# Two stacked transformer blocks on one core: the full stop between projections and recurrence of each later layer taken out, its semaphores cleared in two groups instead

## What is computed

```python
def second_block(x, ...):
    for l in range(DEPTH_2):                                   # 2 layers
        h = rmsnorm(x, g_pre_mix[l])
        y = token_mixer(h, w_in[l], ...)
        x = x + rmsnorm(y, g_post_mix[l])
        h = rmsnorm(x, g_pre_ffn[l])
        y = conv_ffn(h, w_up[l], ffn_conv_w[l], w_down[l])
        x = x + rmsnorm(y, g_post_ffn[l])

def token_mixer(h, w_in, ...):
    z = h @ w_in
    mq, mk, mv, mo, mif, aq, ak, av = split(z)
    qk = silu(causal_dwconv([mq, mk], qk_conv_w) + qk_conv_b)
    log_i, log_f = gates(mif + gate_bias)
    ht = mlstm(q, k, v=mv, log_i, log_f)                       # recurrence with decays
    m_out = rms(ht) * mh_norm_g * sigmoid(mo)
    a_out = sliding_window_attention(rope(aq), rope(ak), av, sinks)
    return [m_out, a_out] @ w_out
```

## Time and profile before

| what | us |
|---|---|
| median of 3 executions | 2817.95 |
| lowest and highest | 2817.07, 2821.88 |
| the profiled execution | 2818.63 |
| its span, first to last instruction | 2816.8 |
| PE busy in the span | 2639.3 (94%) |
| DVE, ACT, POOL busy | 1213.9, 878.8, 848.7 |

### The profile page before, as it was taken

How to read it: one execution, slowest core, us unless ns; L and a number is a source line. 1 busy time by engine, 2 the same in 40 slices (tenths; PEclk the granted TensorE clock), 3 DMA queues, 4 the chain that set the end, 5 groups by cost and what they waited for, 6 DMA issues and landing times.

```text
span 2816.8 us, 36700 instructions
## 1 busy us (share of the span) xinstructions
PE 2639.3 (94%) x14324; PEld 1881.7 (67%) x14324; DVE 1213.9 (43%) x2417; ACT 878.8 (31%) x1666; POOL 848.7 (30%) x1166
## 2 busy tenths in 40 slices
PE   8999999999988888888888899999999999999998
PEld 8997777888533333333333367788888887788887
DVE  4333735314733333333333357553341565643422
ACT  3343334323211111111111144543332445433332
POOL 4343343553000000000000043335555435355454
PEclk9999999999999999999999999999999999999999
DMA  4222221335999999999999951122232221122322
GB/s 147 90 91 96 85 74 54 109 105 195 392 427 427 428 428 429 428 429 429 428 429 428 426 177 64 57 90 90 90 104 106 88 98 60 60 90 93 117 90 75
DMA packets 128007, 572.26 MB, mean 203 GB/s; under 512 B 11136, under 2 KB 58624, under 8 KB 102784
## 3 DMA queue, kind: packets, MB, share of 16 engines
q1 hardware_dynamic: 122624, 561.09, 50.2%
q10 hardware_dynamic: 5248, 9.32, 1.1%
HBM read 566.12 MB, written 4.26 MB: 202 GB/s over the span
## 4 chain that ended last, share of the span: by engine, by line
PE 67%; DMA 22%; DVE 6%; ACT 2%; issue 1%; POOL 1%; SPq 0%; POOLq 0%; DVEq 0%; ACTq 0%
PE ps L390 41%; DMA wide<-in_moe_w 15%; PE ps L1462 8%; DMA arena<-in_moe_w 7%; PE ps L1942 4%; PE ps L1921 3%; PE ps L1909 1%; PE ps L1962 1%; PE ps L640 1%; PE ps L604 1%; PE ps L1928 1%; POOL ring_r L347 1%; PE ps L619 1%; PE ps L1242 1%; PE ps L859 0%
## 5 line engine op out<-in xcount | busy, mean ns | idle before, releaser
L347 POOL TENSOR_TENSOR ring_r<-ring,ring_r 128x256 fp32r<-128x256 f32 (+2 forms) x1136 | 830.0, 772 | 1871.7 <-ACT ring_r L330 1871.7
L390 PE MATMUL ps<-xnT_r,ring_r 128*128 128x512 f32 (+1 forms) x1664 | 483.9, 374 | 0.0
L390 PE MATMUL ps<-ring_r,xnT_r 128*128 128x512 f32 (+1 forms) x1360 | 439.3, 394 | 8.1 <-POOL ring_r L347 2.5
L390 PEld LDWEIGHTS ps<-xnT_r,ring_r 128*128 128x128 f32 x1664 | 304.5, 188 | 56.7 <-issue 1.3
L390 PE MATMUL ps<-ring_r,arena_r 128*128 128x512 f32 x1392 | 327.9, 394 | 0.0
L390 PEld LDWEIGHTS ps<-ring_r,xnT_r 128*128 128x128 f32 x1360 | 285.6, 222 | 51.3 <-issue 7.1
L390 PE MATMUL ps<-xn_r,ring_r 128*128 128x512 f32 (+1 forms) x832 | 310.2, 373 | 0.0
L390 PEld LDWEIGHTS ps<-ring_r,arena_r 128*128 128x128 f32 x1392 | 263.1, 190 | 58.8 <-issue 3.7
L330 ACT ACTIVATE ring_r<-ring 128x1024 fp32r<-128x1024 f32 (+2 forms) x284 | 272.1, 1025 | 93.4 <-DMA ring<-in_w_down 69.4
L1942 PE MATMUL ps<-wide,arena 128*32 128x512 f32 x768 | 203.6, 678 | 92.2 <-DMA wide<-in_moe_w 92.2
L1942 PEld LDWEIGHTS ps<-wide,arena 128*32 128x32 f32 x768 | 55.3, 121 | 237.4 <-issue 237.4
(11 more groups left out here) (386 smaller groups left out, 3475.1 us busy)
## 6 DMA issues: line engine op xcount, KB each, us to landing
wide<-in_moe_w SPq DMA_DIRECT2D x143, 2048.0 KB, 32.9
arena<-in_moe_w SPq DMA_DIRECT2D x47, 2048.0 KB, 32.9
ring<-in_w_in SPq DMA_DIRECT2D x22, 2048.0 KB, 8.3
ring<-in_w_up SPq DMA_DIRECT2D x20, 2048.0 KB, 8.6
ring<-in_w_down SPq DMA_DIRECT2D x10, 2048.0 KB, 7.9
ring<-in_w_in SPq DMA_DIRECT2D x16, 512.0 KB, 4.9
ring<-in_w_out SPq DMA_DIRECT2D x4, 2048.0 KB, 8.3
ring<-in_w_ret_branch SPq DMA_DIRECT2D x2, 2048.0 KB, 8.2
```

The costliest lines, as they stand in the source:

```text
L347: ins = nc.gpsimd.tensor_tensor(ring_r[:, q % 2, piece], ring[:, q % 2, piece], ring_r[:, 2 + q % 2, piece].bitcast(F32), ALU.subtract)
L390: ins = nc.tensor.matmul(bank, left, right, start=(start and k == 0), stop=(stop and k == 2))
```

## The change

The stage semaphores that the later layers use are put in two groups, PROJECTING (34 names, those of the projections) and MIXING (33 names, those of the recurrence and the feed-forward part); the rest is never cleared again. The stop is gone. POOL clears the group that is not in use, twice for each layer but the first:

- in l = 1, after first_low_pool and ahead of the low halves of unit 1, it clears MIXING. It waits until PE has made the second chunk of the first job, ACT has drained behind the second turned tile, and DVE has drained behind enter_dve;
- in both layers, after the low halves of unit 6 and ahead of those of unit 7, it clears PROJECTING, when the three engines have each counted early in the recurrence.

At the start of the recurrence PE now waits for single banks and values instead: rotated keys kept, the last job in bank 7 and in banks 0 and 1 taken, the silu of q and k done, and the low half of the turned attention output. DVE waits for the sigmoid and drains behind the first decay mask, ACT waits for DVE's last taking and drains behind its first exp. wait_cleared (a wait and a count) stands at the head of each part, for groups that were cleared long before.

```diff
-        def next_stage(eng, me, chain=None):
...
-                for done in stage_done.values():
-                    eng.wait_ge(done, n + 1)
-                eng.sem_inc(stage_left, 1)
-                eng.sem_clear(range(nums[0], nums[-1] + 1))
-                eng.drain().then_inc(stage_open, 1)
-            else:
-                eng.drain().then_inc(stage_done[me], 1)
-                eng.wait_ge(stage_open, n + 1)
-                eng.sem_inc(stage_left, 1)
...
+        def clear_left(pool, n, group):
+
+            for done in stage_done.values():
+                pool.wait_ge(done, n)
+            pool.sem_inc(stage_left, 1)
+            pool.sem_clear(group)
+            pool.drain().then_inc(stage_open, 1)
+
+        def wait_cleared(eng, n):
+
+            eng.wait_ge(stage_open, n)
+            eng.sem_inc(stage_left, 1)
...
@@ chunk_pe
+            elif n == 0 and c == 1 and current["l"]:
+                ins.then_inc(stage_done["pe"], 1)
...
@@ project_dve
             enter_dve(v, link)
+            if current["l"]:
+                v.drain().then_inc(stage_done["dve"], 1)
             v.wait_ge(layer_loaded, (current["l"] + 1) * (16 * LAYER_ROWS))
...
@@ project_act
+                    if k == 1 and current["l"]:
+                        a.drain().then_inc(stage_done["act"], 1)
...
@@ a_product_pe
             if c == 0 and n >= 2:
                 pe.wait_ge(V.taken_act, n - 1)
+            elif c == 0:
+                projected_bank_taken(pe, n)
...
+            elif n == 2 and c == 0:
+                ins.then_inc(stage_done["pe"], 1)
...
@@ mlstm_pe
                 elif what == "decays":
                     if k >= 2:
                         pe.wait_ge(Z.strip_ready, k - 1)
+                    elif k:
+                        projected_bank_taken(pe, DECAY_BANKS[1])
+                    else:
+                        pe.wait_ge(Z.turned_kept, 2 * NT)
...
                     if done:
                         pe.wait_ge(V.scores_taken, done)
+                    else:
+                        pe.wait_ge(qk_silu_done, 1)
+                        pe.wait_ge(Z.out_low, NT)
...
@@ mlstm_dve, diagonal
+                if n == 0:
+                    v.wait_ge(mo_sigmoid_done, 1)
+                    v.drain().then_inc(stage_done["dve"], 1)
...
@@ mlstm_act
+            a.wait_ge(Z.taken_dve, max(taken_count(n) for n in range(len(J.order)) if not by_act(n)))
             nc.scalar.activation(floor, floor, ACT.Exp).then_inc(V.exp_ready, 1)
+            a.drain().then_inc(stage_done["act"], 1)
...
@@ the order of POOL
                 if l:
                     first_low_pool(pool)
-                for q in (1, 2, 3, 4, 5):
+                    clear_left(pool, 2 * l + 1, mixing_nums)
+                for q in range(1, Q_UP):
                     low_pool(pool, q)
-                nxt()
-                for q in range(6, LAYER_UNITS):
+                clear_left(pool, 2 * l + 2, projecting_nums)
+                for q in range(Q_UP, LAYER_UNITS):
                     low_pool(pool, q)
```

More of the change, by code:

```diff
@@ L181, in build @@
         STAGE = [
[L182 to L192, removed]
@@ L193, in build @@
-            "x_turned", "x_kept",
-            "act_high", "act_low", "block_used", "attended", "half_gated", "rows_normed", "x_returned", "routes_loaded", "merge_asked", "merge_ready", "out_turned", "out_kept", "out_low", "head_done", "x_low", "ff_ready", "ff_weighted", "ff_taken", "ff_gated", "ff_done",
+            "dve_chain", "act_chain", "expert_x_kept", "last_products", "last_kept", "last_added", "spill_done", "spill_open", "gate_ready",
+            "silu_ready", "up_ready", "hidden_ready", "down_ready", "gate_kept", "up_kept", "gate_summed", "up_summed", "gate_turned",
@@ new lines, in build @@
+            "up_turned", "y_act", "y_dve", "shifted", "picked", "picks_ready", "gated_ready", "gathered", "picks_turned", "picks_kept", "united",
+            "tile_united", "spill_x_kept", "logits_ready", "gains_ready", "spilled_out", "spilled_in", "half_gated", "rows_normed", "x_returned",
+            "routes_loaded",
+        ]
+        PROJECTING = [
+            "attended", "biased", "exp_asked", "exp_ready", "max_ready", "mixed_ready", "mixed_taken", "out_kept", "out_low", "out_turned",
+            "probs_kept", "probs_ready", "probs_turned", "proj_ready", "ranked", "roots_ready", "roped", "rows_ready", "scores_ready",
+            "scores_taken", "sums_ready", "taken_act", "taken_dve", "tile_added", "turned", "turned_kept", "weighted", "x_kept", "x_low",
+            "x_turned", "merge_asked", "merge_ready", "gated", "chosen",
+        ]
@@ L195, in build @@
+        MIXING = [
+            "act_high", "act_low", "block_used", "deviation", "ff_ready", "ff_weighted", "ff_taken", "ff_gated", "ff_done", "head_done",
+            "moments", "strip_asked", "strip_ready", "tile_down", "turned_low",
         ]
@@ L199, in build @@
         ]
-        STAGE += ["later_" + name for name in LATER]
+        MIXING += ["later_" + name for name in LATER]
+        STAGE += PROJECTING + MIXING
         for name in STAGE:
@@ L209, in build @@
         decay_row_ready, queries_weighed = (stage_sems[n] for n in ("ff_gated", "ff_done"))
+        projecting_nums = range(stage_sems[PROJECTING[0]].num, stage_sems[PROJECTING[-1]].num + 1)
+        mixing_nums = range(stage_sems[MIXING[0]].num, stage_sems[MIXING[-1]].num + 1)
+        qk_silu_done, mo_sigmoid_done = stage_sems["gated"], stage_sems["chosen"]
         spill_known = sem("spill_known")
@@ L2538, in layers_sp @@
                     load_small_rows(sp, l + 1)
+            wait_cleared(sp, 2 * LAYERS)
             for i in range(NT):
@@ L2804, in project_act @@
                     if q == Q_MO and i == NT - 1:
-                        nc.scalar.activation(Y.qk, Y.qk, ACT.Silu)
+                        nc.scalar.activation(Y.qk, Y.qk, ACT.Silu).then_inc(qk_silu_done, 1)
                     if q == Q_MV and i == 0:
                         a.wait_ge(Z.taken_act, NT)
-                        nc.scalar.activation(Y.mo, Y.mo, ACT.Sigmoid)
+                        nc.scalar.activation(Y.mo, Y.mo, ACT.Sigmoid).then_inc(mo_sigmoid_done, 1)
                 elif what == "scores":
@@ L2918, in build, with projected_bank_taken @@
         M_TURN_BANK = 7
+        def projected_bank_taken(pe, bank):
+            wait_job_taken(pe, max(n for n in range(len(J.order)) if dense_bank(n) == bank))
         def a_product_pe(pe, n, c):
@@ L3023, in mlstm_pe @@
                         pe.wait_ge(V.mixed_taken, k)
+                    else:
+                        pe.wait_ge(Z.mixed_taken, NT)
                     for i in range(NT):
@@ L3537, in _ @@
                 current["l"] = l
+                if l:
+                    wait_cleared(pe, 2 * l)
                 project_pe(pe)
-                nxt()
+                if l:
+                    wait_cleared(pe, 2 * l + 1)
                 mlstm_pe(pe)
@@ L3560, in _ @@
                 current["l"] = l
+                if l:
+                    wait_cleared(v, 2 * l)
                 project_dve(v, link)
-                nxt()
+                if l:
+                    wait_cleared(v, 2 * l + 1)
                 mlstm_dve(v, link)
@@ L3565, in _ @@
                 down_split_dve(v)
+            wait_cleared(v, 2 * LAYERS)
             last_dve(v, link)
@@ L3619, in _ @@
                 current["l"] = l
+                if l:
+                    wait_cleared(a, 2 * l)
                 project_act(a)
-                nxt()
+                if l:
+                    wait_cleared(a, 2 * l + 1)
                 mlstm_act(a)
@@ L3625, in _ @@
                 down_split_act(a)
+            wait_cleared(a, 2 * LAYERS)
             last_act(a)
```

17 lines of the change are left out of this document (removed).

## The result

| | median us | lowest, highest | ratio to before, 95% interval |
|---|---|---|---|
| before | 2817.99 | 2817.07, 2821.88 | |
| the changed kernel | 2829.32 | 2827.74, 2832.05 | 1.0039 [1.0029, 1.0049] |

The change makes the kernel 0.39% slower; the medians differ by 11 us. The profiled execution of the changed kernel took 2827.84 us with a span of 2825.7.

A forecast was written before the change was run, and what follows sets the result against it. PE was taken to bound the kernel (two thirds of the span), most of the rest being the first block's expert weights. Stops -7.8 and hold +10.8 gave +3.0 us: median 2821.0 us, range 2817.5 to 2826.0.

The forecast's parts named there:

- rival 3: At the recurrence the new waits end as late as the removed stop, which gives nothing: 2828.8 us; chance 0.05.
- No second stall.: In l = 1, behind the first AKV job, POOL is ahead again with QK (11.35 us for four quarters); no cost added.
- POOL's pace: In l = 1, POOL's sixteen AKV pieces behind the new clear take 8.1 us.
- The stops, -7.8: Removing the stops at the recurrence in l = 0 and l = 1 gives 3.9 us each; bounds -3.7 and -7.8.
- Rival 1: Behind the missing stops PE's clock stays low, so two give 3.7 us, not 7.8: 2825.0 us; chance 0.19.
- The hold, +10.8: In l = 1 the new clear holds POOL ahead of AKV: +8.5 late, +2.3 of clock, bounds 8.7 to 12.7.
- the quick end: In l = 1, POOL's sixteen AKV pieces beside an idle DVE take 7.9 us, making the sum 0.2 us lower.
- The clock's 2.3 us: In l = 1, around PE's wait for AKV, half clock costs +2.3 us, bounds 0.7 and 3.4.
- Rival 2: POOL or PE slack hides the wait ahead of AKV in l = 1; only stops count: 2810.2 us; chance 0.09.

The follow-up runs named there:

- the three variants: Changed kernel with the l = 1 clear of MIXING behind QK, behind unit 5, or behind QK plus PSUM operand: 2815.80, 2813.57, 2812.31 us.
- the two kernels without the long add: Changed kernel with the keys' sine term in PSUM, or with POOL pausing ahead of QK until DVE's first AKV rotary step: 2820.62, 2821.11 us.

## Why the prediction was wrong, step by step

The time, 2829.3, lies above the range of 2817.5 to 2826.0. Of the chances, slower by over 0.2% had 0.30; it came, but not by the mechanism that I had given it. That rival 3's 2828.8 lies near the measured time is chance: its mechanism, a stop under another name, is not in the profile.

**The step that failed is "No second stall."** I asked whether POOL's pieces of QK would be in time for PE, and they were. I didn't ask what DVE had to do meanwhile. Before, there was a pause of 4.66 us between AKV and QK, and DVE's adds for the keys came through the run behind it in 0.29 to 0.81 us. Pushed together into one run of 17.75 us, the pieces kept out, for 8.68 us, the add that PE's transposes of the keys wait for. The hold at the earlier trace rows moved POOL's work on top of DVE's, and only POOL's pace was priced for that (8.1 us), not DVE's. In the measurements this step is worth 8.1 to 8.5 us to the second scores (159.6 against 151.1 and 151.5), of which PE's wait is 6.4 and the clock about 1.7. Without it the kernels stand at 1.0008 and 1.0010, 2820.6 and 2821.1 us, and the forecast was 2821.0. That this fits is partly luck: the hold cost some 3 us less than forecast, and the stops gave less in the medians than forecast, and the two errors cancel.

The rule of the Trainium skill ("SBUF — State Buffer", section "SBUF: two separate sides") that I weighed for POOL's pace speaks to exactly this: a DVE op with two SBUF inputs and a GpSimd op that reads SBUF exclude each other, and the loser blocks. I used one side of it. The trace agrees on which op is hit (8.68 us with two SBUF operands, 0.29 with one in PSUM). That section of the Trainium skill has the lock held for one instruction. By my estimate from it and from the length of a piece, the add would have waited 0.7 us at most; here it waited through twelve pieces. So the section, read for DVE, would have pointed to the place, but not to the size.

**The stops, -7.8.** The mechanism and its sizes to the second scores were right: 3.8 and 3.7 us measured, 3.9 forecast, half of it the clock. Rival 1 (the clock stays low) falls as put: with PE kept busy the clock held. It lives on in small, as a fall in some executions that costs 0.4 to 0.9 us. Of the whole, the three variants show less in the medians: 0.12% [0.03%, 0.21%], 0.15% [0.06%, 0.25%] and 0.21% [0.11%, 0.30%], that is 3.4 to 5.9 us. Only the last interval reaches 7.8. Their profiled executions gained 7.2 to 7.8. Which share of the difference is the fall of the clock, the later waits or the first block stays open.

**The hold, +10.8.** POOL's first piece came 29.1 us behind the first product, as forecast (2259.6 - 2230.39 = 29.2). The clear took 0.22 us. The sixteen pieces took 6.8 us instead of 8.1, with DVE idle; even the 7.9 of the quick end was too much. The first AKV job ended 7.7 us late, forecast 8.5. The clock's 2.3 us were counted on top, and that was the mis-sized term: the clock was low while PE waited for each quarter of POOL anyway, and in the two kernels without the long add it was at full speed from the second job on (1.00 from 2265 to 2280). The hold without the long add measures 7.3 to 7.7 to the second scores.

Together, to the second scores: -3.7 for the second stop, +7.5 for the hold and +8.3 for the add make the +12.1 of l = 1; with -3.8 in l = 0 that is +8.3. The profiled span grew by 8.9, the median by 11.3; where the other 2.4 us of the median come from isn't shown.

**The other rivals.** Rival 2 (the stall is hidden) and rival 3 (the stop under another name) fall by the chains above.

## What to carry to other kernels

When a wait holds an engine back, what follows from it is not only late but also in another place: ask which work of its neighbours the late run will now lie on, and whether one of them can keep the other out. Here it was a break in POOL's run that let DVE work. Where a GpSimd run must lie on such work, one drain in the run or an operand in PSUM bounds the damage (8.7 us to 3.65, and to 0.29). And a clear or another duty without a due time goes behind the work that somebody waits for: the same change with that one line moved is faster than before, by 0.12% to 0.21%.

## What the runs showed of the hardware that was not expected

- A DVE add of 128x128 with both operands in SBUF, 0.29 us alone, was kept out for 8.68 us by back-to-back GpSimd subtractions of 0.68 to 0.70 us each, twelve of which began while it waited; in the kernel before the same add came through a run of the same pieces within 0.81 us. How far the run has come separates the two cases in all twelve profiles. Fifty-three such adds began by the thirteenth piece of an unbroken run, and none took more than 0.88 us. The three that began during the nineteenth or twentieth piece waited for the end of the run (8.68, 9.06 and 3.65 us). Idle time ahead of the run doesn't separate them, since POOL had been idle for 33 us ahead of the run of 32, and a drain of 0.16 us is enough to let DVE in between pieces again. Why the length of the run matters isn't shown.
- The clear of 33 semaphores took 0.22 us, the clear of all of them 0.61.
- PE's clock fell to 1.2 GHz without a pause of PE, behind the decay and score products of 4 and 64 rows, at five of eighteen places (PEclk 0.88 over 14 us instead of 1.00 in the one shown above).
